# Twenty-four modulation rows of one layer: from one VectorE instruction each to a GpSimd product and a ScalarE sum

## The reference, cut to what matters

```python
mod = jax.nn.silu(c) @ w_ada[l] + b_ada[l]          # 1024 -> 6 * 1024
sh1, sc1, g1, sh2, sc2, g2 = jnp.split(mod[:, None, :], 6, axis=-1)
h = rms_norm(x, norm_g[l, 0]) * (1.0 + sc1) + sh1
...                                                 # h @ w_in, mixers A, B, C
mix = jnp.concatenate([o_a, o_b, o_c], axis=-1) @ w_out[l]
x = x + g1 * mix
h = rms_norm(x, norm_g[l, 1]) * (1.0 + sc2) + sh2
x = x + g2 * conv_ffn(h, w_up[l], conv_w[l], conv_b[l], w_down[l])
```

## Time and profile before

| | us |
|---|---|
| median of 3 runs | 2490.69 (2483.61 to 2491.72) |
| the profiled execution | 2489.72 |
| its span in the trace | 2487.9 |
| TensorE busy | 2400.2 (96%) |
| VectorE busy | 1612.6 (65%) |
| ScalarE busy | 847.5 (34%) |
| GpSimd busy | 299.9 (12%) |

### The profile page before, as it was taken

The page is one execution under the profiler, slowest core; times in us unless marked ns, Lnnn a source line. Parts: engine busy times, 40 slices in busy tenths (PEclk is TensorE's granted clock), DMA queues, the critical chain, the costliest instruction groups (busy, mean ns, idle before and its releaser), DMA issues.

```text
span 2487.9 us, 45532 instructions
## 1 busy us (share of the span) xinstructions
PE 2400.2 (96%) x17088; PEld 2226.1 (89%) x17088; DVE 1612.6 (65%) x3756; ACT 847.5 (34%) x2183; POOL 299.9 (12%) x386
## 2 busy tenths in 40 slices
PE   7988999999999999999999999999899999999998
PEld 5858889878888987999999999988589999999998
DVE  6785665574666246795888883325629858888634
ACT  2542120444211123323666540022622246665300
POOL 1030110011110001010111121100301101111210
PEclk9989999999999999999999999999899999999999
DMA  8347879322889555699999999964038989999997
GB/s 329 147 145 283 306 284 344 119 68 103 320 300 359 182 178 186 202 414 349 395 407 400 412 405 414 391 218 134 1 119 295 414 325 408 405 399 413 404 414 296
DMA packets 171487, 727.02 MB, mean 292 GB/s; under 512 B 19152, under 2 KB 19664, under 8 KB 146384
## 3 DMA queue, kind: packets, MB, share of 16 engines
q1 hardware_dynamic: 142992, 521.76, 56.0%
q0 software_dynamic: 27648, 201.34, 20.0%
q10 hardware_dynamic: 704, 2.10, 0.4%
HBM read 721.97 MB, written 1.05 MB: 291 GB/s over the span
## 4 chain that ended last, share of the span: by engine, by line
PE 86%; DVE 7%; DMA 3%; ACT 2%; issue 2%; SPq 0%; DVEq 0%; ACTq 0%
PE banks L744 35%; PE lev L1135 23%; PE banks L1081 22%; PE lev L744 2%; DMA ring<-in_peer_u 1%; PE banks L1062 1%; PE lev L1062 1%; PE banks L854 1%; PE banks L906 1%; DVE arena L1945 1%; ACT arena L1402 1%; DVE arena L2318 1%; DMA arena<-in_ada 0%; DVE arena L1971 0%; DMA extra<-in_ada 0%
## 5 line engine op out<-in xcount | busy, mean ns | idle before, releaser
L744 PE MATMUL banks<-hT,ring 128*128 128x256 f32 (+1 forms) x2832 | 587.5, 369 | 8.8 <-ACT hT L1311 6.4
L744 PEld LDWEIGHTS banks<-hT,ring 128*128 128x128 f32 x2832 | 516.4, 191 | 76.1 <-issue 8.5
L1081 PE MATMUL banks<-hT,ring 128*128 128x160 f32 x4096 | 580.8, 302 | 3.0 <-DMA ring<-in_peer_u 2.9
L1135 PE MATMUL lev<-arena,ring 128*128 x4096 | 576.6, 301 | 0.0
L1081 PEld LDWEIGHTS banks<-hT,ring 128*128 128x128 f32 x4096 | 559.4, 191 | 5.9 <-issue 2.6
L1135 PEld LDWEIGHTS lev<-arena,ring 128*128 128x128 f32 x4096 | 558.9, 191 | 0.0
L1761 POOL DMA_INDIRECT arena<-in_peer_rows,keysb x192 | 185.7, 967 | 1133.9 <-DVE consts L2172 675.8
L744 PE MATMUL banks<-arena,ring 128*128 128x256 f32 (+2 forms) x1648 | 286.4, 336 | 7.4 <-issue 6.1
L744 PEld LDWEIGHTS banks<-arena,ring 128*128 128x128 f32 x1648 | 260.5, 193 | 32.4 <-issue 7.1
L2219 DVE SCALAR_TENSOR_TENSOR extra<-consts,chT 128x192 bf16<-128x192 f32 x640 | 223.7, 408 | 17.8 <-ACT arena L1450 17.7
L2184 DVE CUSTOM_DVE_ANT_0 arena<-arena 128x1024 f32<-128x1024 f32 x64 | 78.2, 1222 | 166.1 <-DMA arena<-in_peer_rows,keysb 166.1
(11 more groups left out here) (282 smaller groups left out, 2252.4 us busy)
## 6 DMA issues: line engine op xcount, KB each, us to landing
ring<-in_peer_u SPq DMA_DIRECT2D x256, 512.0 KB, 9.4
ring<-in_peer_v SPq DMA_DIRECT2D x256, 512.0 KB, 8.5
ring<-in_stream_first SPq DMA_DIRECT2D x188, 512.0 KB, 5.3
arena<-in_ada SPq DMA_DIRECT2D x104, 512.0 KB, 5.6
extra<-in_ada SPq DMA_DIRECT2D x88, 512.0 KB, 5.3
ring<-in_stream_nsa SPq DMA_DIRECT2D x45, 512.0 KB, 3.4
ring<-in_stream_fox SPq DMA_DIRECT2D x41, 512.0 KB, 3.6
arena<-in_peer_rows,keysb POOLq DMA_INDIRECT x192, 8.6
```

The lines of the kernel that those rows point to most:

```text
L744: ins = nc.tensor.matmul(o, lhsT, rhs, start=start, stop=stop, **kw)
L1081: ins = nc.tensor.matmul(banks[k // 2 % 4][:, (k % 2) * ND:(k % 2 + 1) * ND], ring[:, u % RING, c], hT[:, c, NS:T], start=c == 0, stop=c = ...
L1135: ins = nc.tensor.matmul(lev[c // 4][:, (c % 4) * T + NS:(c % 4 + 1) * T], ring[:, u % RING, c], a[:, bass.ds(g, 1), k], start=False, stop ...
```

## The change

Row loads of layer 0 are spread: four behind unit 12, two each behind units 18, 20, 22 and 24, twelve behind unit 26. For rows 16 to 39 GpSimd multiplies the tile by silu(c) in place (`scale_ada`), and ScalarE copies it onto itself with an accumulator output, which is the sum (`sum_ada`). VectorE leaves them out, and waits once for all forty before `mods(0, 2, 5)`. GpSimd does rows 16 to 23 ahead of the rotary products, 24 to 29 behind them, and one ahead of each of attention units 0 to 9. ScalarE sums two rows in each of steps 4, 5, 6, 7 and 10 of the projections, two in attention steps 0 and 1, and one in steps 2 to 11.

```diff
+import itertools
...
@@ -619,7 +620,10 @@
         ADA_TURNS = [[24] + [2] * FC + [8, 8, 8, 0], [0] + [2] * 16 + [3] * 6 + [6, 6, 6, 0]]
-        ADA_LEVELS, ADA_UNITS, ADA_OUT = [4, 0], [[0] * 4 + [1] * 6 + [2] * 2, [0] * NATT], [(5, 5, 4, 0), (0, 0, 0, 0)]
+        ADA_LOADS = {12: 4, 18: 2, 20: 2, 22: 2, 24: 2, 26: 12}
+        SUMMED = range(16, 40)
+        SUMS_IN, SUMS_ATT = {4: 2, 5: 2, 6: 2, 7: 2, 10: 2}, [2, 2] + [1] * 10
+        assert sum(ADA_LOADS.values()) == len(SUMMED)
         EARLY = 2 * DEPTH * ADA
@@ -693,10 +697,8 @@
                         sp.dma_start(crow[:, 1], io["c_rows"][:, 1]).then_inc(sem("c2_in"), 16)
-                    if k == RING + 6:
-                        load_ada(ADA_LEVELS[l])
-                    if k == U_IN + 5:
-                        load_ada(ADA_TURNS[l][0] - ADA_LEVELS[l])
+                    if l == 0:
+                        load_ada(ADA_LOADS.get(k, 0))
                     at = k - (U_IN + U_OUT)
@@ -1392,6 +1394,8 @@
                         u, nk = u0 + step, keys_of(us[step])
+                        if u < NATT:
+                            sum_ada(SUMS_ATT[u])
                         if not biased[u]:
@@ -1503,6 +1507,16 @@
                 weights(dots_at(2 * GATES - 1), NR)
+
+            summed = iter(SUMMED)
+
+            def sum_ada(k):
+
+                for n in itertools.islice(summed, k):
+                    ch = ada_row(n)
+                    wait(sem("ada_scaled"), n - SUMMED[0] + 1)
+                    A(ada_slot(n), ada_slot(n), ACT.Copy, accum_out=mod[:, 0, ch // DC, ch % DC:ch % DC + 1])\
+                        .then_inc(sem("ada_used"), 1)
@@ -1565,6 +1579,8 @@
                         decay(l, k - 5)
+                    if l == 0:
+                        sum_ada(SUMS_IN.get(k, 0))
                 def outputs_B():
@@ -1721,10 +1737,11 @@
-            def attention(name, us, u0):
+            def attention(name, us, u0, scaled=()):
                 for k in range(len(us)):
...
                     nk = keys_of(us[k])
+                    scale_ada(scaled[k:k + 1])
                     pool.wait_ge(sem("rinv_ready"), u + 1)
@@ -1736,13 +1753,22 @@
                 G.tensor_tensor(hT[:, c], xT[:, c], rstd[:, :], ALU.mult).then_inc(sem("h_scaled"), 1)
+            def scale_ada(ns):
+
+                for n in ns:
+                    pool.wait_ge(sem(f"ada_in{n % ADA_RING}"), 16 * ((n - 16) // ADA_RING + 1))
+                    G.tensor_tensor(ada_slot(n), ada_slot(n), crow[:, 0], ALU.mult).then_inc(sem("ada_scaled"), 1)
+
             pool.wait_ge(sem("consts_in"), 16)
+            scale_ada(SUMMED[:8])
             for l in range(DEPTH):
...
                     G.tensor_tensor(x2, x2, cos.unsqueeze(1).broadcast_to([P, 2, T]), ALU.mult).then_inc(sem("cos_done"), 1)
-                attention(("att", l), units_of(l), l * NATT)
+                if l == 0:
+                    scale_ada(SUMMED[8:14])
+                attention(("att", l), units_of(l), l * NATT, SUMMED[14:] if l == 0 else ())
                 for k in range(FC):
@@ -1789,7 +1815,7 @@
                                                scalar=0.0, op0=ALU.mult, op1=ALU.add,
-                                               accum_out=mod[:, l, ch // DC, ch % DC:ch % DC + 1]), "ada_used")
+                                               accum_out=mod[:, l, ch // DC, ch % DC:ch % DC + 1]), sem("ada_used"), n + 1)
                     ada_n[0] += 1
@@ -2028,12 +2054,14 @@
-                attention(("att", l), units_of(l), l * NATT, ADA_UNITS[l],
+                attention(("att", l), units_of(l), l * NATT, None,
                           {0: lambda: None if l == 0 else roots_C(3), 1: lambda: roots_C(0), 2: lambda: roots_C(1), 3: lambda: roots_C(2), 4: norm_C, NATT + 2: lambda: roots_B(0), NATT + 3: lambda: roots_B(1)})
...
                 if l == 0:
-                    mods(0, 2, 3)
-                residual(2 * l + 1, ("out", l), l, 2, ADA_OUT[l], None if l else lambda: mods(0, 3, 5))
+                    ada_n[0] = SUMMED[-1] + 1
+                    wait(sem("ada_used"), ada_n[0])
+                    mods(0, 2, 5)
+                residual(2 * l + 1, ("out", l), l, 2)
                 for k in range(FC):
```

## The result

The changed kernel took 2494.92 us (median of 20 runs, 2486.99 to 2501.82) against 2488.56 for the kernel before (20 runs, 2479.09 to 2492.57). The ratio is 1.0029, 95% interval 1.0020 to 1.0037: it is slower by 5 to 9 us. I had forecast 2488 and no difference.

A forecast was written before the change was run, and what follows sets the result against it. It took the chain of waits as bound by VectorE in projections and attention, then a late weight load in the residual; -9.0 + 8.7 - 1.5 = -1.8 us from 2489.72 gave 2487.9, taken 2488, range 2480 to 2498.

The forecast's parts named there:

- -9.0: Residual term: layer 0's 42.8 us falls to layer 1's 33.8 if units 26 and 27 arrive in time.
- +8.7: Projections term, 5.5 to 13.5: reciprocal 8.0 us late, plus 0.7 for later products meeting VectorE.
- -1.5: Attention term: first to last probabilities 31.3 us against 33.4, with 0.6 given back for turns.
- instructions with two SBUF inputs: Projections: only such GpSimd and VectorE instructions take turns, each meeting costing 1.5 to 2.1 us.
- the 7.0 to 9.1 worked out: Projections: lateness of the chain at the reciprocal in us, taken 8.0, with ends of 5.5 and 11.
- the row's 0.77: Projections: us lost by a VectorE difference beside a GpSimd product of 1.09, scaled in proportion to 1.5.
- The late pair: End of projections: products of rows 28 and 29 meet the last levels on VectorE, 0 to 2.5 us, taken 0.7.
- the square behind the two sums: Projections: ScalarE's statistics square follows the sums of rows 16 and 17, ending at 74.0 against 65.2.
- low end of 5.5: Projections: reciprocal 5.5 us late with no turns, only the two rows' landing and products delaying.
- The 0.6 us for turns: Attention: GpSimd taking turns with the few two-input VectorE instructions gives back 0.6 us.
- the slower rival: Whole kernel: GpSimd products take 2.9 us, giving +7.7 and 2497; decides past about 2.3 us; chance 0.18.
- The rival by which unit 27 still waits: Residual: unit 27 and later loads still wait, the 6.09 us gap stays, total +7, 2497; chance 0.05.

The follow-up runs named there:

- e3: The changed kernel without ScalarE's sums of rows 16 to 25, GpSimd's products kept; 2494.03 us in a single run.
- e5: The changed kernel with ScalarE's sums of rows 16 and 17 moved behind the square and the next bank's decays; 2500.70 us in a single run.
- e2: The changed kernel without GpSimd's products of rows 16 to 25, ScalarE's sums kept; 2482.87 us in a single run.
- e4: The changed kernel without GpSimd's products of rows 30 to 39, those between attention units; 2496.38 us in a single run.
- e7: The changed kernel with each product of rows 16 to 29 cut into four instructions of 256 columns; 2501.03 us in a single run.
- e11: The changed kernel without GpSimd's products of rows 28 and 29; 2493.97 us in a single run.
- e1: The kernel before with only the late row loads split behind weight units 25 and 27, products and sums on VectorE; 2480.72 us against 2487.16, ratio 0.9969.
- e8: The kernel before with the loads split and rows 16 to 19 multiplied by GpSimd behind the rotation, summed by ScalarE; 2479.55 us against 2488.25, ratio 0.9964.

## Why the prediction was wrong

The measured 2494.92 lies inside the range of 2480 to 2498, but it moved up where the sum had it go down by 1.8. The three stages were right, and so was the mechanism, instructions of GpSimd and VectorE that hold each other up; the sizes were not, and in the projections neither was the engine that the reciprocal waits for. The sum had -9.0, +8.7 and -1.5. The profile has -7.4, +13.0 and 0.0, and 0.5 from an earlier start of before's run that has nothing to do with the change: together +6.1, where the second half of the up projection is 6.3 us later and the medians 6.4 apart. The projections are 4.3 of the miss, the residual 1.6, attention 1.5.

**The projections: the step that failed.** I took +8.7 with 5.5 to 13.5, and 13.0 was measured: 10.4 up to the reciprocal where I had 8.0, and 2.7 behind it where I had 0.7. It was mis-sized at four places.
- Which instructions of VectorE wait. The prediction let only "instructions with two SBUF inputs" take turns, since the earlier trace rows showed that pair, and let products 17 to 19 delay the differences "to between 74 and 77". The copies, with one input, waited as well, 2.0 us each. They do 1024 columns in 0.69 us where a difference needs 1.23. The Trainium skill (SBUF — State Buffer, section "SBUF: two separate sides") names VectorE's instructions in a two-port performance mode beside those with two inputs; the copies fit that, and I had weighed the rule without this half. The differences ran from 77.0 to 79.5, and behind them L2044 and L2045 met the next pair. The reciprocal was 10.4 us late (after the mark), beyond the 7.0 to 9.1 worked out and near the high end of 11.
- How long one wait is. I put it at 1.5 to 2.1 us; the copies lost 1.98 and 2.03, the scans 3.93 together, L2045 2.16. That is the whole product but for what had passed when they came. In the earlier trace rows the difference came 0.24 us behind the product's start, so its 0.77 was a remainder, and scaling it in proportion had no ground. The part of the Trainium skill's rule that I priced at 9.1 (one instruction waits out the other) was nearer than the row's 0.77.
- What the reciprocal waits for. I let it follow ScalarE's sums, drain, table and roots (8.3 us from the decays on). It followed VectorE, whose L2044 and L2045 had met the next pair of products (9.12 us); the roots were ready 1.05 us earlier.
- The late pair. I took 0.7 with 0 to 2.5; it measured 2.1. The other 0.5 us behind the reciprocal are 0.4 in the tiles, at a clock of 0.50 against 0.53, and 0.15 ahead of the pair.

What I had described in most detail, the square behind the two sums, came out to 0.3 us (it ended at 73.7, forecast 74.0) and was worth nothing: e3 and e5 took it off the path, and the end of the stretch didn't move. Two chains led to the first decays: ScalarE had its table loaded at 75.0, VectorE had its difference ready at 78.2. I had worked out both, to 75.2 and to between 74 and 77, and spent most of the working on the one that does not count. The low end of 5.5, "no turns", was off as well: without the early products, and so with no turns, e2 has the reciprocal 2.9 us late.

**Attention.** Forecast 31.3, measured 33.4. The product takes 2.35 us and not 2.1, which is nine times 0.25, or 2.3 us. The 0.6 us for turns were right in kind: one pair of products for the probabilities took 1.80 instead of 0.93. My price came from the two shapes of the earlier trace rows, 0.72 and 1.09 us at 256 and 512 columns; 1024 columns take more than twice the 512, so a line through short shapes was too low, and even the double of the longer one was. The estimate of 2.25 us from the Trainium skill (GPSIMD Engine Reference, section 3.1) was closer than my own, and the trace is 0.1 above it. I had named 2.3 us as the point from which the slower rival decides; with 2.35 the sum by my own rule would have been about +0.5. That the measured +6.4 lies near that rival's +7.7 is chance: its attention of 38.5 us did not come (33.4), and its +11 for the projections came out at 13.0 with the shorter product.

**The residual.** Forecast 33.8 us, measured 35.5 in this profile; in e2, e4, e5, e7 and e11, which have the changed kernel's loads, 33.9, and in e3 35.4. The 1.6 us goes with TensorE's clock in a part of the runs. Windows of 16 us about the end of attention, of the changed kernel and then of e4 (PE, PEld, DVE, ACT, POOL busy; granted clock; DMA):

```profile
176.00:192.00 16.00, 13.66 (x74) 11.17 (x75) 7.19 (x14) 8.85 (x14) 0.98 (x3) 0.79 0.21 67
```

```profile
176.00:192.00 16.00, 13.90 (x87) 11.20 (x83) 7.51 (x13) 8.16 (x12) 0.33 (x1) 1.00 0.29 97
```

e3 shows 0.79 in this window too, and e2, e5, e7 and e11 1.00: the two kinds of runs fall apart exactly as their 35.4 and 33.9 us do. 0.79 is a mean over the two levels of 1.2 and 2.4 GHz: in the changed kernel it is 0.50 from 179.6 to 185.6 us, and in e4 1.00 over the same instructions. Why the lower one was granted in the one kind was not tested. The rival by which unit 27 still waits is out: no wait of TensorE for a load is left.

**What was not seen at all.** The gain of 9.0 was booked to the change as a whole. It belonged to one part of it, the place of the loads (e1: 8.2 us by `up`, about 6 in the medians), which costs nothing. For the 13.0 us paid in the projections the only return would have been in attention, where GpSimd took over as the bound. Had I asked of each part what it alone is worth, the change would have fallen into a part worth -8 and a part worth +14.

## What to carry to other kernels

When a change does two things, price them apart: here moving the loads gave 8 us in the first layer and moving the arithmetic took 14 back. Work given to GpSimd was paid by VectorE where its scans, copies and two-input instructions met a product, with up to one whole product each; the long reciprocal was not held up (6.55 us beside two products at 87.37, as before). So such work belongs where VectorE is off the critical path: four rows behind the rotation cost about 1.4 us and saved 5 in attention. The count of such VectorE instructions in the stretch prices it, not GpSimd's idle time. Where two chains meet, compute both arrivals, at each meeting point, before spending the working on one of them. And where a difference of one or two microseconds between single profiles is to carry a claim, lay the granted clock of the same instructions beside it first: 2.3 us of e11 and the whole cost of the four rows were hidden in it.

## What the hardware showed that I had not expected

- A copy of 64x1024 with one input took 2.67 us beside a product on GpSimd and 0.69 without; a predicated copy from the level's PSUM bank took 1.32 us beside one at 132.72, as it does alone.
- Who is held up differed with the length of the pieces. Chained products of 2.35 us alternate with VectorE's instructions one for one. Quarters of 0.69 us were slowed by a full queue of VectorE (eight in 9.11 us), and held one instruction of VectorE back for all the quarters left in a row of eight (4.92 us instead of 1.22).
- A product of 128x256 takes GpSimd 0.69 us and one of 128x1024 2.35, so four quarters cost 2.76.
- With products in the projections two profiles of nearly the same instructions differ by 2.2 us up to the first exponential; without, three profiles lie within 0.2.
- The same 40 matmul records ahead of the first exponential, tiles and scores, took 8.24 us at a granted clock of 0.53 and 6.40 at 0.96 (before and e8).
